# Low parts of the down projection's activations made by GpSimd, and eight row passes moved from the gate spreading to the down projection

## The reference, cut to what matters

```python
# per token t, 8 heads, 16 experts picked for each head out of 16384
eidx = ...            # numbers of the picked experts
g = softmax(top)      # their gates
u = u_tab[eidx]       # rows of a 16384 x 1024 table
v = v_tab[eidx]       # rows of a second 16384 x 1024 table
a = gelu(einsum('thkd,td->thk', u, h))
out = einsum('thk,thkd->td', g * a, v)
```

## Time and profile before

| | |
|---|---|
| median of 3 runs | 1424.04 us (1423.16 to 1425.38) |
| the profiled execution, its own time | 1425.08 us |
| its span in the trace | 1423.3 us |
| TensorE busy over the span | 1389.8 us (98%) |
| VectorE, ScalarE, GpSimd busy | 1128.2, 779.7, 367.0 us |
| DMA | 363.40 MB, 255 GB/s on average |
| last instruction of the down projection's matmuls | 1411 us |

### The profile page before, as it was taken

How to read it: one execution, slowest core, us unless ns; L and a number is a source line. 1 busy time by engine, 2 the same in 40 slices (tenths; PEclk the granted TensorE clock), 3 DMA queues, 4 the chain that set the end, 5 groups by cost and what they waited for, 6 DMA issues and landing times.

```text
span 1423.3 us, 28089 instructions
## 1 busy us (share of the span) xinstructions
PE 1389.8 (98%) x10819; PEld 1296.3 (91%) x10819; DVE 1128.2 (79%) x2293; ACT 779.7 (55%) x1580; POOL 367.0 (26%) x423
## 2 busy tenths in 40 slices
PE   8899999998999999999999999899999999999998
PEld 7678998877889988898899999899999999999998
DVE  5776996787768889867657998576677699999997
ACT  6875886853355555567464202244343366666665
POOL 7700001000200000001100124697877432222220
PEclk9999999999999999999999999999999999999999
DMA  7305554651369999843444699999999999999993
GB/s 265 99 16 185 175 170 147 193 179 61 136 213 352 306 332 350 283 159 94 137 135 148 193 376 355 357 352 356 367 348 360 381 368 362 358 338 362 359 357 127
DMA packets 100274, 363.40 MB, mean 255 GB/s; under 512 B 11168, under 2 KB 11296, under 8 KB 100016
## 3 DMA queue, kind: packets, MB, share of 16 engines
q1 hardware_dynamic: 68096, 245.71, 49.6%
q0 software_dynamic: 24272, 88.64, 17.0%
q10 hardware_dynamic: 7776, 27.27, 5.3%
HBM read 360.52 MB, written 1.05 MB: 254 GB/s over the span
## 4 chain that ended last, share of the span: by engine, by line
PE 83%; DVE 10%; ACT 3%; DMA 2%; issue 2%; POOL 1%; DVEq 0%; ACTq 0%
PE ps L662 81%; DVE arena L1404 3%; DMA arena<-in_u_rows,arena 2%; DVE w_lo L1404 2%; DVE arena L2177 1%; ACT arena L2321 1%; ACT w_hi L2324 1%; PE ps L880 1%; PE ps L1007 0%; PE ps L837 0%; DVE arena L2014 0%; DVE arena L2011 0%; ACT arena L2324 0%; DVE arena L2012 0%; POOL arena L3245 0%
## 5 line engine op out<-in xcount | busy, mean ns | idle before, releaser
L1404 DVE TENSOR_TENSOR w_lo<-arena,w_hi 128x512 fp32r<-128x512 f32 x680 | 459.0, 690 | 148.1 <-ACT w_hi L2324 143.2
L2324 ACT ACTIVATE w_hi<-arena 128x512 fp32r<-128x512 f32 x680 | 422.0, 626 | 270.7 <-PE ps L662 256.7
L662 PE MATMUL ps<-act_hi_lo,w_hi 128*128 128x256 f32 (+1 forms) x2496 | 550.4, 314 | 3.5 <-DVE w_lo L1404 2.1
L662 PE MATMUL ps<-arena 128*128 128x176 f32 (+7 forms) x4780 | 477.8, 281 | 15.7 <-issue 4.4
L662 PEld LDWEIGHTS ps<-arena 128*128 128x128 f32 (+3 forms) x4780 | 452.0, 165 | 36.5 <-issue 18.8
L662 PE MATMUL ps<-act_hi_lo,w_lo 128*128 128x176 f32 (+1 forms) x1760 | 455.5, 259 | 0.1
L662 PEld LDWEIGHTS ps<-act_hi_lo,w_hi 128*128 128x128 f32 x2496 | 420.6, 190 | 8.6 <-issue 4.5
L662 PEld LDWEIGHTS ps<-act_hi_lo,w_lo 128*128 128x128 f32 x1760 | 336.1, 191 | 0.1
L662 PE MATMUL ps<-w_hi,act_hi_lo 128*128 128x512 f32 (+2 forms) x960 | 301.3, 389 | 7.9 <-DVE w_lo L1404 3.1
L1404 DVE TENSOR_TENSOR arena<-arena 128x512 f32<-128x512 f32 (+18 forms) x308 | 183.6, 605 | 68.9 <-ACT arena L2321 63.6
L662 PEld LDWEIGHTS ps<-w_hi,act_hi_lo 128*128 128x128 f32 x960 | 179.4, 188 | 50.2 <-issue 10.2
(11 more groups left out here) (104 smaller groups left out, 667.5 us busy)
## 6 DMA issues: line engine op xcount, KB each, us to landing
arena<-in_w_ff SPq DMA_DIRECT2D x128, 512.0 KB, 4.1
arena<-in_peer_u SPq DMA_DIRECT2D x128, 512.0 KB, 6.3
arena<-in_peer_v SPq DMA_DIRECT2D x128, 512.0 KB, 6.8
arena<-in_w_ada ACTq DMA_DIRECT2D x48, 512.0 KB, 5.5
arena<-in_w_glu SPq DMA_DIRECT2D x16, 512.0 KB, 4.2
arena<-in_peer_wq SPq DMA_DIRECT2D x16, 512.0 KB, 3.6
arena<-in_w_in SPq DMA_DIRECT2D x12, 512.0 KB, 4.5
arena<-in_w_conv SPq DMA_DIRECT2D x12, 512.0 KB, 4.2
```

What stands on the lines that cost most here:

```text
L662: return e.matmul(o, l, r, start=start, stop=stop)
L1404: return e.tensor_tensor(o, a, b, op)
L2324: return e.activation(o, a, ACT.Copy)
```

## The change

GpSimd, which issued only gathers in the down projection, now makes the low parts of the activations of groups 1 to 63 too, by the same subtraction on 128x352; VectorE keeps that of group 0. TensorE waits for GpSimd's signal (`alo_pool`) in place of VectorE's. GpSimd's order in the stage is written out: for each j, wait for ScalarE's high part of group j+1, make its low part, then issue the gathers whose passes n-4 lie at or before step 4j+3. `N_LATE` goes from 100 to 92: eight row passes fewer are spread over the gate spreading, and 68 in place of 60 over the down projection.

```diff
-    N_PASS, N_FIRST, N_BETWEEN, N_LATE, N_ONES = len(passes), 16, 23, 100, 3
+    N_PASS, N_FIRST, N_BETWEEN, N_LATE, N_ONES = len(passes), 16, 23, 92, 3
...
# tensor_program, down_T
                         if m == 0 and hf == 0:
-                            e.wait_ge(*alo_cut[name, j])
+                            e.wait_ge(*(alo_pool if j else alo_cut)[name, j])
...
# down_T_last
-            e.wait_ge(*alo_cut[name, 63])
+            e.wait_ge(*alo_pool[name, 63])
...
# vector_program, down
-                        if m == 0 and hf == 0 and j + 1 < units // 2:
+                        if m == 0 and hf == 0 and j + 1 < units // 2 and name != "peer_v":
                             cut_pair(name, j + 1, src_of(j + 1))
...
# gpsimd_program
-        for n in range(N_LATE + 3, N_PASS):
-            gather(n)
+        n = N_LATE + 3
+        for j in range(63):
+            hi, lo = [x[:, :, 0:ND] for x in HQ[(j + 1) % 4]]
+            e.wait_ge(*ahi_cut["peer_v", j + 1])
+            tt(lo, X[:, 2 * j + 2:2 * j + 4, :], hi.bitcast(F32), ALU.subtract).then_inc(*alo_pool("peer_v", j + 1))
+            while n < N_PASS and (n - 4 < N_LATE or pass_step(n - 4) <= 4 * j + 3):
+                gather(n)
+                n += 1
+        assert n == N_PASS
```

## The result

The changed kernel takes 1448.16 us (median of 5 runs, 1446.67 to 1453.31) against 1424.33 before (5 runs); the ratio is 1.0171, with an interval of 1.0157 to 1.0185. Slower was forecast, but by 6 us, not by 24, and 1448 lies outside the range.

A forecast was written before the change was run, and what follows sets the result against it. TensorE bounds the kernel; in the down projection the port shared by VectorE and GpSimd would become the bound. 7 us for it, 2 for lateness, less 3 at the gate spreading: 6 us slower, 1430 us, range 1419 to 1440.

The forecast's parts named there:

- What bounds the kernel: Gate spreading from 950 us and down projection: TensorE is the bound, 4.335 us per group of four chunks; VectorE's work is hidden.
- The loads of VectorE: Down projection, VectorE's cost each: low weights 0.60 us, low activations 0.44, a row pass 1.20.
- the way to add them: Down projection: VectorE's costs and closed time summed per group, 4.45 us, against TensorE's 4.335; the larger is the bound.
- the price of the closed time: Down projection: each GpSimd low part keeps VectorE's two-input operations out for 0.74 us, scaled from 0.54.
- the upper bound of 0.95: Down projection: closed time at most the whole GpSimd operation, 0.95 us, making the load 4.66 us a group and costing 20 us.
- The mechanism, reading by both engines: Down projection: two-input VectorE instructions and GpSimd instructions reading SBUF take turns; the second issued is blocked.
- GpSimd's order: Down projection: low parts queued behind gathers come late for passes at step 3; ten stalls of 0.2 us, 2 us.
- GpSimd is late: Rival, chance 0.13: down projection low parts late behind gathers for step 2 passes too, 19 us less 3: 1440.
- The eight passes: Moved into the down projection: 1.31 us of VectorE a group for passes, 4.2 MB more fetched there.
- the DMA's edge: Down projection: the added fetches need 369 GB/s, a DMA share of 1.01; costs 0 to 3 us unless the stage lengthens.
- The gate spreading: Its start, 890 to 940 us: fewer fetches cut TensorE's 5.9 us of idle time by 3, bounds 0 and 5.9.
- The sum: Whole kernel: 7 + 2 - 3 = 6 us above the profiled execution's 1425.1.

The follow-up runs named there:

- e1: Kernel before with only the eight row passes moved (`N_LATE` 92), VectorE making all low parts; ratio 0.9992.
- e5: Kernel before, unchanged, profiled once more; a single run, 1428.54 us.
- e6: Kernel before with sixteen row passes moved (`N_LATE` 84, 76 in the down projection), VectorE making all low parts; ratio 0.9989.
- e11: Same kernel as e6, timed again with more rounds; ratio to the kernel before 0.9972.
- e3: Changed kernel, but GpSimd clears one column and waits for it before each low part, keeping it apart from the gathers; ratio to before 1.0088.
- e7: e3 with `N_LATE` back at 100, so 60 passes in the down projection; ratio to before 1.0038.
- e4: Changed kernel with GpSimd's subtraction replaced by a write-only zero fill, same order and signals; ratio to before 0.9998.
- e8: e3, but GpSimd makes the low part of one unit of each pair and VectorE that of the other; ratio to before 1.0066.
- e10: e9 with `N_LATE` back at 100, so 60 passes in the down projection; ratio to before 1.0012.
- e9: Changed kernel with gathers for passes at step 2 or 3 of a group issued after the next low part, no clearing; ratio to before 1.0086.
- e2: Changed kernel with `N_LATE` back at 100: GpSimd makes the low parts, 60 passes in the down projection; ratio to before 1.0101.

## Why the prediction was wrong

**What bounds the kernel** held. e1, e5, e6 and e11 keep TensorE busy in all 260 us, and what VectorE does up to 4.30 us a group is hidden.

**The loads of VectorE** (0.60, 0.44 and 1.20 us) held, and where VectorE makes all low parts so did the way to add them: 4.15 and 4.30 us cost nothing (e1, e6). With GpSimd's order in the path the sum of averages is only the least that the stage takes: e3 (4.28) and e7 (2.40 + 1.15 + 0.46 = 4.01) stay under 4.335 and lose 10.7 and 6.7 us.

**The step that failed is the price of the closed time**, "0.54 x 352/256 = 0.74 us". It was taken from GpSimd operations that stood alone or behind operations of their own kind. For a low part that stands alone it is right: 0.69 to 0.75. But in the changed kernel nearly all stand right behind a gather, and most of these cost 1.16 (40 of 48 over 1.0), over the upper bound of 0.95 that I had thought to be the whole instruction. With the average of all, 56.0 us over 54 low parts, 1.04, the sum is 2.40 + 1.31 + 1.04 = 4.75 us a group against 4.79 measured: 62.5 x (4.75 - 4.335) = 26 us, and 26.5 was measured. The missing term is 62.5 x 0.30 = 19 us. The order of the work on GpSimd, which the prediction wrote out for the lateness alone, was also what set this price.

**The mechanism, reading by both engines, held** (e4), and so did its sign. As the Trainium skill has it (SBUF — State Buffer, "Who interferes with whom"), GpSimd's write-only fill didn't contend. That one is blocked for the other's whole instruction is true within 0.2 us at its end: a low weight that was held ended 0.55 us after the low part, and it takes 0.68, so it got through some 0.13 us before the low part's recorded end; a pass, by the same count, 0.19.

**GpSimd's order**: 2 us were forecast. In e7 lateness was all of the 6.7 us, with 60 passes; at e8's long gathers, with the clock that fell after them, it was most of the loss. The rival "GpSimd is late" was no rival but a second part. How much of it is in the changed kernel's 26.5 us isn't shown: TensorE waited for GpSimd for 4.4 us there, and the load alone already gives 26.

**The eight passes**: the DMA's edge (0 to 3 us) cost nothing, in e11 not even at 379 GB/s.

**The gate spreading**: -3 us. In the profiled execution the stretch was shorter by 4.2 us (256.7 to 252.5), but the average over six profiles is 1.5. The step took idle time of one execution for a property of the kernel. It had no term for the clock, which in e1, e4, e5 and e10 cost 1.7 us there.

**The sum** in measured terms: +26.5 in the down projection, -4.2 in the gate spreading, -0.8 in what lies before it (the first one-hot at 876.1 in place of 876.9): 21.6 us, the difference of the spans 1444.9 and 1423.3. Beyond that the medians differ by 2 us more: the profiled execution of the changed kernel was the fastest of its five, 1.5 us under their median, and that of the kernel before lay 0.8 over its own.

## What to carry to other kernels

An engine that looks free isn't, if its reads keep the busy one out: count GpSimd's elementwise work with two-input VectorE instructions as VectorE's time, 0.69 to 0.75 us for 128x352 here, where VectorE's own instruction for it cost 0.44. Look at what stands in front of such an instruction in its engine's own queue, and price it in that position (up to 1.2 us here). A load under the bound is not enough either, if the engine's order makes a result late. And before an idle stretch of a few microseconds goes into a sum, see whether a second execution has it.

## What the runs showed of the hardware

A two-input GpSimd instruction right behind a gather can keep VectorE out while the gather is still recorded as running. Two VectorE instructions start within the gather of 1163.54 us: the first, at 1163.79, takes its usual 0.68 us; the second, at 1164.39, 0.31 before the gather's end, takes 1.83. All 84 closed times over 1.0 us are of this kind: the held instruction starts 0.26 to 0.33 us before the gather's end. Where VectorE's instruction starts 0.3 us after that end, 0.74 us are added. In front of a low part that finds GpSimd idle, or stands behind the clearing, VectorE instructions that start 0.1 to 0.4 us before it keep their lengths. Clearing one column and waiting for it, 0.11 us, takes the effect away. The Trainium skill says (GPSIMD Engine Reference, "2.1 Instruction dispatch") that a core of GpSimd starts the next instruction as soon as its own share of the last is done, whatever the other cores do. By that rule cores that are through with the gather would take the interface before the low part's recorded start. The runs fit this and don't show the single cores, so it stays argued; nor does it say why the time is 0.3 us.

How long a gather keeps GpSimd isn't fixed: the median is 1.15 us in the down projection of the kernel before, e1 and e4 (354 to 373 GB/s), but 2.10 in e6 and 2.35 in e11 (381 and 379 GB/s, 76 passes), with single ones up to 3.61. Whether the traffic or the closer passes do it, the runs don't separate. It harms nobody unless something stands behind it.

In the window from 910 to 920 us, after idle stretches of TensorE between 900 and 920, the mean granted clock was 0.83 in e1, e4, e5 and e10, that is the lower of the two levels (1.2 GHz) for a third of it; in the other profiles it stayed at 1.00. The length of the idle stretch alone doesn't tell which: it fell after one of 2.02 us in e10 and after 2.76 to 2.90 in e1, e4 and e5, and stayed after one of 2.44 in e9; the kernel before stood idle for 5.9 us in four pieces, the longest 2.16, and kept it. So the full clock was not granted throughout in every run: in e2's and e8's down projections it was half for some microseconds behind a stall, and in the kernel before from 1420.8 us to the end, behind its last large matmuls. In e1 the 10 us held 42 matmuls in place of 73 at full pace. Half the clock for 3.4 us costs 1.7, and e1's idle time from 890 to 940 us is 2.0 longer than the changed kernel's (4.1 against 2.1): 3.7 of the 3.8 us by which its stretch is longer (256.3 against 252.5), with the same passes.
